# Moving the scaled and biased logits of a stick-breaking attention from ScalarE to VectorE

## The chip, the cores and the metric

The kernel runs on one core of one Trainium2 chip. The metric is the device time of one execution in microseconds (us), as the median of several executions. Engine names in the profile: PE is TensorE, DVE is VectorE, ACT is ScalarE, POOL is GpSimd, SP is SyncE.

## The reference

One inference step of a decoder with two layers, for 512 prompt tokens and 32 new tokens of 8 sequences, all in float32. Layer 0 is a recurrent block, layer 1 an attention block. The change touches only the attention over the prompt, which in the reference is:

```
z = einsum('bqkgd,bskd->bkgqs', qb, k) / sqrt(HEAD_DIM)      # HEAD_DIM = 128
z = z + bias[None, :, :, None, None]                          # one bias per head
mask = kpos[None, :] < qpos[:, None]                          # strictly causal
log_keep = where(mask, log_sigmoid(-z), 0.0)
suffix = cumsum(log_keep, axis=4, reverse=True) - log_keep
attn = where(mask, exp(log_sigmoid(z) + suffix), 0.0)
o = einsum('bkgqs,bskd->bqkgd', attn, v)
```

There are 16 heads in 4 groups (k = 0..3) of 4 heads (g = 0..3) that share one key and value head.

## The kernel before

**Tiling.** Every dense matrix product is done in three float32r passes (weights high x input high, high x low, low x high). The weights come in units of eight 128x128 tiles (512 KB). For each unit SP issues the DMA into `raw`, POOL multiplies it by the gain of a norm (`fold`, L633), ACT rounds it to a high part (`high`, L1197), DVE takes the rest as the low part (`low`, L1647), and PE multiplies the unit. `raw` and `WS` have two slots: SP may load a slot again when the `low` of that slot is done, so the time of a `low` sets the time of a later DMA and with it of a later `fold`. A unit takes PE about 6 us when nothing is put in between.

**The attention stage.** Loop `for n in range(D_UNITS)` runs over 64 weight units of the layer-1 projections. The 64 attention steps over the prompt are put in between by hand: a step is (k, g, s), where s = 0..3 picks one block of 128 keys, from the last to the first, and the queries from `FIRST_Q[s]` on: 256, 256, 384 and 512 of them. Sixteen steps of one k fall on 14 units from n = 7 + 14k on, most units with one step; the units n = 13 + 14k and n = 16 + 14k hold two, (s = 2, s = 3), and are called double units here. Inside a unit PE has a fixed place for each part of a step: the query-key product of the step after (`qk`) and the second part of the running sum (`rest`) in the first third, or after the first and the fifth tile in a double unit; the value product of the step before (`pv`, L912 to L914) and the running sum (`later`, L890 and L891) at the end, or in the middle and at the end of a double unit.

**One step** goes through the engines so:

- PE: `qk` writes the raw logits to `Z[:, 0, s % 2]` in PSUM.
- ACT, `exp_logits`: T1 = |scale z + bias| (L1377), T0 = scale z + bias (L1378), both read from PSUM; then T1 = exp(-T1) (L1380) and T1 = ln(1 + T1) (L1381).
- DVE, `softplus`: T3 = min(T0, 0) - T1 (L1934), T2 = max(T0, 0) + T1 (L1935), and a mask on T2 (L1937).
- ACT, `sp_split` (L1407), and DVE, `sp_rest` (L1942): high and low part of T2, which PE's `later` sums.
- DVE, `exponent` (L1948): T3 minus the sum in PSUM. ACT, `exp_arg` (L1389): exp of it. DVE, `mask_weights` (L1953). ACT, `at_split` (L1397), and DVE, `at_rest` (L1958): high and low part of the weights, which PE's `pv` takes.

**The order is written out by hand on each engine.** On ACT a step is `exp_arg` of the step before; for s = 0 `exp_logits` of this step; `at_split` of the step before; `sp_split`; and for s < 3 `exp_logits` of the next step. On DVE it is:

```
                if before:
                    exponent(*before)
                if next_unit is not None:
                    low(D0 + next_unit, next_unit % 2)
                if before:
                    mask_weights(*before)
                if s == 1 and (k or g):
                    head_out(*((k, g - 1) if g else (k - 1, GRP - 1)))
                softplus(k, g, s)
                if before:
                    at_rest(*before)
                sp_rest(k, g, s)
```

In an even unit DVE first takes the finished strip of the projection out of PSUM (`strip`, L1975 to L1978 or L1990); after the step come the low parts of a query or key strip (`q_rest`, L2010, `k_rest`, L2015), and in some odd units the gate product `silu` (L2001 to L2005). `gate_sigmoid` on ACT (L1443) loads another table set before and after its activation (the loads are at L1443 and L1445). It stands ahead of the step in n = 8 + 14k, and, for the gate strips behind the heads, in n = 58, 60 and 62. Behind the last step (n = 63) the paged decode attention begins, with its own logits (`logits`, L2079: scale and bias of a 128x512 PSUM tile on DVE).

Of the kernel before, what the change touches and what calls it, by code (L numbers as in the profile page):

```python
# [26 lines left out]
ALU = mybir.AluOpType  # L27
ACT = mybir.ActivationFunctionType
# [4 lines left out]
SEQ = 512  # L33
# [12 lines left out]
NH, NKV, GRP = 16, 4, 4  # L46
# [4 lines left out]
SCALE = DH ** -0.5  # L51
# [75 lines left out]
def build(nc, a, out):  # L127
    ctx = ExitStack()
    with ctx:
        def sem(name):  # L130
            return ctx.enter_context(nc.semaphore(name))
# [4 lines left out]
        def sb(name, shape, dt=F32, offset=None):  # L136
            size = 4
            for n in shape[1:]:
                size *= n
            if offset is None:  # L140
                offset = at[0]
                at[0] += (size + 31) // 32 * 32
            return nc.alloc_sbuf_tensor_at(name, list(shape), dt, offset=offset), offset
# [8 lines left out]
        T, T_AT = sb("T", [P, 12, 572])  # L152
# [10 lines left out]
        BIAS, _ = sb("BIAS", [P, NH])  # L163
# [34 lines left out]
        Z = ctx.enter_context(nc.psum_tensor("Z", [P, 2, 2, 512], F32))  # L198
# [6 lines left out]
        bias_in = sem("bias_in")  # L205
# [17 lines left out]
        sgb_ready = sem("sgb_ready")  # L223
        silu_done = sem("silu_done")
        qk_done = sem("qk_done")
        z_abs = sem("z_abs")
        z_out = sem("z_out")
        l_ready = sem("l_ready")
        sp_ready = sem("sp_ready")
# [164 lines left out]
        FIRST_Q = (2 * P, 2 * P, P, 0)  # L394
# [794 lines left out]
        def _(act):  # L1189
# [17 lines left out]
            steps = Steps(act, act_step)  # L1207
# [161 lines left out]
            def exp_logits(k, g, s):  # L1369

                n = k * 16 + 4 * g + s
                q = slice(FIRST_Q[s], SEQ)
                act.wait_ge(qk_done, n + 1)
                if n:
                    act.wait_ge(sp_ready, n)
                bias = BIAS[:, k * GRP + g:k * GRP + g + 1]
                nc.scalar.activation(T[:, 1, q], Z[:, 0, s % 2, q], ACT.Abs, scale=SCALE, bias=bias).then_inc(z_abs, 1)  # L1377
                nc.scalar.activation(T[:, 0, q], Z[:, 0, s % 2, q], ACT.Identity, scale=SCALE, bias=bias).then_inc(z_out, 1)  # L1378
                act.wait_ge(z_abs, n + 1)
                steps.done(nc.scalar.activation(T[:, 1, q], T[:, 1, q], ACT.Exp, scale=-1.0))  # L1380
                nc.scalar.activation(T[:, 1, q], T[:, 1, q], ACT.Ln, bias=1.0).then_inc(l_ready, 1)  # L1381

# [64 lines left out]
            def step(k, g, s):  # L1447
                before = (k, g, s - 1) if s else (k, g - 1, 3) if g else (k - 1, GRP - 1, 3) if k else None
                if before:
                    exp_arg(*before)  # L1450
                if s == 0:
                    exp_logits(k, g, 0)
                if before:
                    at_split(*before)
                sp_split(k, g, s)
                if s < 3:
                    exp_logits(k, g, s + 1)
# [45 lines left out]
                act.wait_ge(silu_done, GATES.index((o // GRP, o % GRP)) + 1)  # L1503
                nc.scalar.activation(U[:, o, 0:SEQ], Y[:, o, 0:SEQ], ACT.Copy).then_inc(y2_high, 1)

            act.wait_ge(bias_in, 16)
            for n in range(D_UNITS):
                j = n - PAGES_AT
                if 0 <= j < NHALF:
# [12 lines left out]
                kind, k, g = STRIPS[n // 2 - 1] if n >= 2 and n % 2 == 0 else (None, 0, 0)  # L1522
# [117 lines left out]
        def _(dve):  # L1640
            steps = Steps(dve, dve_step)
            V = nc.vector

            def low(m, slot, tiles=UT):

                dve.wait_ge(w_high, m + 1)
                V.tensor_tensor(WS[:, slot, 1, 0:tiles, :], raw[:, slot, 0:tiles, :],  # L1647
                                WS[:, slot, 0, 0:tiles, :].bitcast(F32), ALU.subtract).then_inc(w_low, 1)
# [271 lines left out]

            later_sum, o_sum = Z[:, 1, 0], Z[:, 1, 1]

            def masked_part(tile, s):

                q0 = FIRST_Q[s]
                return (tile[:, q0:q0 + 2 * P], MSK[:, :]) if s == 0 else (tile[:, q0:q0 + P], MSK[:, P:2 * P])

            def softplus(k, g, s):

                n = k * 16 + 4 * g + s  # L1930
                q = slice(FIRST_Q[s], SEQ)
                dve.wait_ge(l_ready, n + 1)
                dve.wait_ge(z_out, n + 1)
                V.scalar_tensor_tensor(T[:, 3, q], T[:, 0, q], 0.0, T[:, 1, q], ALU.min, ALU.subtract)  # L1934
                steps.done(V.scalar_tensor_tensor(T[:, 2, q], T[:, 0, q], 0.0, T[:, 1, q], ALU.max, ALU.add))  # L1935
                part, mask = masked_part(T[:, 2], s)
                V.tensor_tensor(part, part, mask, ALU.mult).then_inc(sp_ready, 1)  # L1937

            def sp_rest(k, g, s):
                q = slice(FIRST_Q[s], SEQ)  # L1940
                dve.wait_ge(sp_high, k * 16 + 4 * g + s + 1)
                V.tensor_tensor(U[:, 37, q], T[:, 2, q], U[:, 36, q].bitcast(F32), ALU.subtract).then_inc(sp_low, 1)  # L1942

            def exponent(k, g, s):

                q = slice(FIRST_Q[s], SEQ)
                dve.wait_ge(later_done, k * 16 + 4 * g + s + 1)
                V.tensor_tensor(T[:, 3, q], T[:, 3, q], later_sum[:, q], ALU.subtract).then_inc(arg_ready, 1)  # L1948

            def mask_weights(k, g, s):  # L1950
                dve.wait_ge(at_exp, k * 16 + 4 * g + s + 1)
                part, mask = masked_part(T[:, 4], s)
                V.tensor_tensor(part, part, mask, ALU.mult).then_inc(at_masked, 1)  # L1953

            def at_rest(k, g, s):
                q = slice(FIRST_Q[s], SEQ)
                dve.wait_ge(at_high, k * 16 + 4 * g + s + 1)
                V.tensor_tensor(U[:, 39, q], T[:, 4, q], U[:, 38, q].bitcast(F32), ALU.subtract).then_inc(at_low, 1)  # L1958

            def head_out(k, g):  # L1960

                dve.wait_ge(pv_done, k * 16 + 4 * g + 4)
                y = Y[:, k * GRP + g, 0:SEQ]
                if g:
                    V.tensor_copy(y, o_sum).then_inc(o_out, 1)
                else:
                    V.tensor_tensor(y, y, o_sum, ALU.mult).then_inc(o_out, 1)
# [53 lines left out]
            def step(k, g, s, next_unit):  # L2021
                before = (k, g, s - 1) if s else (k, g - 1, 3) if g else (k - 1, GRP - 1, 3) if k else None
                if before:
                    exponent(*before)
                if next_unit is not None:
                    low(D0 + next_unit, next_unit % 2)
                if before:
# [4 lines that stand above are left out]
                if before:  # L2032
                    at_rest(*before)
                sp_rest(k, g, s)
            def key_copy(c):
                dve.wait_ge(kp_t, c + 1)
                if c >= 4:
                    dve.wait_ge(kp_used, c - 3)
                V.tensor_copy(KPT[:, c % 4, :], KT).then_inc(kp_odd, 1)  # L2039
# [60 lines left out]
            for n in range(D_UNITS):  # L2100
# [3 lines left out]
                kind, k, g = STRIPS[n // 2 - 1] if n >= 2 and n % 2 == 0 else (None, 0, 0)  # L2104
# [3 lines left out]
                for t, step_ in enumerate(STEPS_AT.get(n, ())):  # L2108
                    step(*step_, next_unit if t == 0 else None)
# [16 lines left out]
                if 0 <= j < NHALF:  # L2126
                    key_copy(4 * j + 1)
# [14 lines left out]
                if 0 <= j < NHALF:  # L2142
                    key_copy(4 * j + 3)
                    logits(j)
# [115 lines left out]
```

## Time and profile before

| | |
|---|---|
| time, median of 3 executions | 1854.16 us (1853.96 to 1854.96) |
| time of the profiled execution | 1854.96 us |
| span of the profiled execution, first to last instruction | 1853.1 us |
| PE busy | 1741.2 us, 94% |
| DVE busy | 1095.8 us, 59% |
| ACT busy | 841.8 us, 45% |
| POOL busy | 250.4 us, 14% |
| attention steps over the prompt | 940 to 1418 us of the span |

The profile is of one execution. Busy time is a union of the instructions' times on an engine. A matmul is pipelined: one takes some 290 ns from start to end, and the next starts some 125 ns after it at full clock. The number in brackets behind a row of the timeline is how long the engine had been idle before the instruction, and whose end ended it.

### The profile page before, as it was taken

The page shows a single profiled execution, that of the slowest core. Times are in us where ns is not written, and L with a number is a line of the kernel's source. Part 1 is how long each engine was busy: PE and PEld are TensorE (multiplying, and loading weights), DVE is VectorE, ACT ScalarE, POOL GpSimd, SP SyncE. Part 2 cuts the span into 40 slices and gives each one's busy share as a digit, 9 for nine tenths or more (in the row PEclk, how much of TensorE's full clock was granted, in tenths as well). Part 3 has the DMA queues.
Part 4 walks back from the last instruction along what each step waited for, and adds up shares of the span by engine and source line. Part 5 has one row for each costly group of instructions (what it writes and reads, how often), then busy time and mean ns, then how long its engine had stood idle before and what let it go on. Part 6 is the DMA issues. An engine that isn't in the chain of part 4 may idle for free.

```text
span 1853.1 us, 35499 instructions
## 1 busy us (share of the span) xinstructions
PE 1741.2 (94%) x14003; PEld 1673.6 (90%) x14003; DVE 1095.8 (59%) x1853; ACT 841.8 (45%) x1310; POOL 250.4 (14%) x189
## 2 busy tenths in 40 slices
PE   6999999999999999994799999999988999999997
PEld 5999999999999999993698998998987888899995
DVE  4766555676557422229667677676676666642366
ACT  4434444334446222223256566665665555722343
POOL 2000000000000000013332232322311111001111
PEclk9999999999999999995699999999999999999997
DMA  8322332332332322334221222222223777622465
GB/s 243 109 86 75 90 91 81 88 102 70 89 91 57 91 85 85 90 115 144 88 82 59 57 83 58 80 69 58 81 57 100 213 225 222 200 76 84 135 185 181
DMA packets 293525, 197.97 MB, mean 107 GB/s; under 512 B 8379, under 2 KB 267579, under 8 KB 293307
## 3 DMA queue, kind: packets, MB, share of 16 engines
q1 hardware_dynamic: 290632, 187.36, 34.8%
q0 software_dynamic: 2720, 8.78, 1.3%
q8 instruction: 68, 1.11, 0.3%
q10 hardware_dynamic: 68, 0.41, 0.1%
q14 instruction: 37, 0.30, 0.1%
HBM read 180.55 MB, written 15.97 MB: 106 GB/s over the span
## 4 chain that ended last, share of the span: by engine, by line
PE 81%; DVE 9%; issue 4%; ACT 3%; DMA 1%; SPq 0%; POOL 0%; ACTq 0%; DVEq 0%
PE PS L722 23%; PE PS L724 23%; PE PS L723 23%; PE Z L972 2%; PE Z L722 2%; PE Z L724 1%; PE Z L723 1%; PE Z L982 1%; DMA xin<-in_x_prompt_dram 1%; DVE WS L1647 1%; PE Z L1006 1%; DVE T L1935 1%; DVE T L1934 1%; DVE Y L1903 1%; DVE U L1910 1%
## 5 line engine op out<-in xcount | busy, mean ns | idle before, releaser
L722 PE MATMUL PS<-U,WS 128*128 128x272 f32 x3680 | 1082.9, 294 | 48.2 <-DVE U L1910 34.1
L724 PE MATMUL PS<-U,WS 128*128 128x272 f32 x3680 | 1072.1, 291 | 0.0
L723 PE MATMUL PS<-U,WS 128*128 128x272 f32 x3680 | 1069.6, 291 | 0.0
L722 PEld LDWEIGHTS PS<-U,WS 128*128 128x128 f32 x3680 | 700.9, 190 | 61.1 <-issue 27.3
L723 PEld LDWEIGHTS PS<-U,WS 128*128 128x128 f32 x3680 | 701.6, 191 | 0.8
L724 PEld LDWEIGHTS PS<-U,WS 128*128 128x128 f32 x3680 | 700.8, 190 | 0.0
L1647 DVE TENSOR_TENSOR WS<-raw,WS 128x1024 fp32r<-128x1024 f32 (+1 forms) x223 | 272.3, 1221 | 381.4 <-ACT WS L1197 378.8
L1197 ACT ACTIVATE WS<-raw 128x1024 fp32r<-128x1024 f32 (+1 forms) x225 | 230.8, 1026 | 495.5 <-PE PS L724 492.0
L633 POOL TENSOR_TENSOR raw<-raw,GN 128x1024 f32<-128x1024 f32 x80 | 156.2, 1954 | 535.3 <-DMA raw<-in_b_w_in_dram 456.0
L645 POOL TENSOR_TENSOR T<-T 128x544 f32<-128x544 f32 x39 | 54.6, 1400 | 307.8 <-ACT T L1336 307.8
L642 POOL COPY T<-T 128x544 f32<-128x544 f32 x3 | 2.4, 791 | 623.2 <-ACT T L1336 573.8
L1407 ACT ACTIVATE U<-T 128x256 fp32r<-128x256 f32 (+1 forms) x64 | 32.0, 499 | 63.9 <-DVE T L1937 63.9
L1948 DVE TENSOR_TENSOR T<-T,Z 128x256 f32<-128x256 f32 (+1 forms) x64 | 33.2, 518 | 35.8 <-PE Z L891 35.1
L1397 ACT ACTIVATE U<-T 128x256 fp32r<-128x256 f32 (+1 forms) x64 | 31.7, 495 | 48.8 <-DVE T L1953 48.8
L1465 ACT ACTIVATE KPT<-Z 128x512 f32<-128x512 f32 x32 | 19.1, 598 | 74.7 <-PE Z L972 74.7
L2039 DVE COPY KPT<-Z 128x512 f32<-128x512 f32 x32 | 22.1, 691 | 50.4 <-PE Z L972 50.2
L1744 DVE SCALAR_TENSOR_TENSOR T<-T,CH 128x512 f32<-128x512 f32 x60 | 45.1, 752 | 7.7 <-DVE T L1742 2.6
L1336 ACT ACTIVATE T<-Y 128x544 f32<-128x544 f32 (+1 forms) x42 | 27.2, 647 | 48.7 <-DVE Y L1875 48.6
L724 PE MATMUL Z<-U,GWS 128*128 128x272 f32 x160 | 46.0, 288 | 0.0
L722 PE MATMUL Z<-U,GWS 128*128 128x272 f32 x160 | 45.9, 287 | 0.0
L723 PE MATMUL Z<-U,GWS 128*128 128x272 f32 x160 | 45.8, 286 | 0.0
L972 PE MATMUL Z<-IDN,KPG 128*128 128x128 f32 x256 | 41.9, 286 | 0.9 <-DMA KPG<-in_cache_k_dram 0.9
(284 smaller groups left out, 2062.2 us busy)
## 6 DMA issues: line engine op xcount, KB each, us to landing
raw<-in_a_w_in_dram SPq DMA_DIRECT2D x80, 512.0 KB, 3.8
raw<-in_b_w_in_dram SPq DMA_DIRECT2D x64, 512.0 KB, 4.1
raw<-in_a_w_out_dram SPq DMA_DIRECT2D x32, 512.0 KB, 3.8
KPG<-in_cache_k_dram SPq DMA_DIRECT2D x64, 256.0 KB, 3.1
raw<-in_b_w_out_dram SPq DMA_DIRECT2D x32, 512.0 KB, 3.9
VPG<-in_cache_v_dram SPq DMA_DIRECT2D x60, 256.0 KB, 3.0
RAW<-in_b_w_out_dram SPq DMA_DIRECT2D x12, 512.0 KB, 4.5
scratch_x<-T POOLq DMA_DIRECT2D x16, 272.0 KB, 3.5
```

Of the source, the lines that this page charges most:

```text
L633: pool.tensor_tensor(raw[:, slot], raw[:, slot], g, ALU.mult).then_inc(w_fold, 1)
L645: ins = pool.tensor_tensor(T[:, 6, 0:TOK], T[:, 6, 0:TOK], sq, ALU.add)
L722: pe.matmul(psum, w_hi, x_hi, start=first, stop=False)
L723: pe.matmul(psum, w_hi, x_lo, start=False, stop=False)
L724: return pe.matmul(psum, w_lo, x_hi, start=False, stop=last)
L972: ins = pe.transpose(KT[:, k * P:(k + 1) * P], KPG[j % 2][:, i, k * DH:(k + 1) * DH], IDN[:])
L1197: nc.scalar.activation(WS[:, slot, 0, 0:tiles, :], raw[:, slot, 0:tiles, :], ACT.Copy).then_inc(w_high, 1)
L1397: nc.scalar.activation(U[:, 38, q], T[:, 4, q], ACT.Copy).then_inc(at_high, 1)
L1407: nc.scalar.activation(U[:, 36, q], T[:, 2, q], ACT.Copy).then_inc(sp_high, 1)
L1647: V.tensor_tensor(WS[:, slot, 1, 0:tiles, :], raw[:, slot, 0:tiles, :], WS[:, slot, 0, 0:tiles, :].bitcast(F32), ALU.subtract).then_inc(w_ ...
L1744: V.scalar_tensor_tensor(xc[:, 0:SEQ], xp[:, k:k + SEQ], param(i, j, k), xc[:, 0:SEQ], ALU.mult, ALU.add)
L1948: V.tensor_tensor(T[:, 3, q], T[:, 3, q], later_sum[:, q], ALU.subtract).then_inc(arg_ready, 1)
```

## The change

T0 = scale z + bias is made by DVE as a `tensor_scalar` (a new function `scaled`), no longer by ACT as an Identity activation. ACT takes the absolute value of T0 in SBUF in place of its own pass over PSUM, and waits for `scaled` (semaphore `z_out`) where it waited for PE (`qk_done`); its exp now waits for its own absolute value just ahead of it. PE still waits for `z_out` before it writes a `Z` buffer again; the count is now raised by DVE. `scaled` for s = 0 stands on DVE behind `exponent` and ahead of `low`; for the other s it stands at the end of the step before, behind `sp_rest`. DVE waits in `scaled` for `qk_done` and for the ln of the step before. The semaphore `z_abs` goes, and so do DVE's wait for `z_out` in `softplus` and ACT's wait for the bias ahead of the loop (DVE has had one).

```diff
@@ scalar, exp_logits
-                act.wait_ge(qk_done, n + 1)
+                act.wait_ge(z_out, n + 1)
                 if n:
                     act.wait_ge(sp_ready, n)
-                bias = BIAS[:, k * GRP + g:k * GRP + g + 1]
-                nc.scalar.activation(T[:, 1, q], Z[:, 0, s % 2, q], ACT.Abs, scale=SCALE, bias=bias).then_inc(z_abs, 1)
-                nc.scalar.activation(T[:, 0, q], Z[:, 0, s % 2, q], ACT.Identity, scale=SCALE, bias=bias).then_inc(z_out, 1)
-                act.wait_ge(z_abs, n + 1)
+                steps.done(nc.scalar.activation(T[:, 1, q], T[:, 0, q], ACT.Abs))
                 steps.done(nc.scalar.activation(T[:, 1, q], T[:, 1, q], ACT.Exp, scale=-1.0))
                 nc.scalar.activation(T[:, 1, q], T[:, 1, q], ACT.Ln, bias=1.0).then_inc(l_ready, 1)
@@ scalar, ahead of the loop
-            act.wait_ge(bias_in, 16)
@@ vector
+            def scaled(k, g, s):
+                n = k * 16 + 4 * g + s
+                q = slice(FIRST_Q[s], SEQ)
+                dve.wait_ge(qk_done, n + 1)
+                if n:
+                    dve.wait_ge(l_ready, n)
+                V.tensor_scalar(T[:, 0, q], Z[:, 0, s % 2, q], SCALE, BIAS[:, k * GRP + g:k * GRP + g + 1],
+                                ALU.mult, ALU.add).then_inc(z_out, 1)
@@ vector, softplus
                 dve.wait_ge(l_ready, n + 1)
-                dve.wait_ge(z_out, n + 1)
@@ vector, step
                 if before:
                     exponent(*before)
+                if s == 0:
+                    scaled(k, g, 0)
                 if next_unit is not None:
                     low(D0 + next_unit, next_unit % 2)
@@ vector, end of step
                 sp_rest(k, g, s)
+                if s < 3:
+                    scaled(k, g, s + 1)
```

## Rows read from the trace of the kernel before

**Rows 1.** The page: span, and busy time of each engine.

```profile
span 1853.1 us, 35499 instructions
PE 1741.2 (94%) x14003; PEld 1673.6 (90%) x14003; DVE 1095.8 (59%) x1853; ACT 841.8 (45%) x1310; POOL 250.4 (14%) x189
```

**Rows 2.** Sums by window: stretch, length, busy PE PEld DVE ACT POOL, PE clock, DMA.

```profile
940.00:1418.00 478.00, 451.19 (x3357) 435.80 (x3360) 329.47 (x611) 301.31 (x557) 123.79 (x79) 0.99 0.25 71
```

**Rows 3.** Waits, 940 to 1418 us: who waited for whom, total us, times, longest.

```profile
PE Z L912 <- DVE U L1958: 14.6, 10, 2.2
...
PE Z L890 <- DVE U L1942: 4.7, 3, 2.8
```

**Rows 4.** One source line, the Identity activation: ns least/median/most.

```profile
L1378 ACT ACTIVATE T<-Z,BIAS x64: 462/518/684, 943.3 to 1404.5; 128x256 f32<-128x256 f32 x32, 128x384 f32<-128x384 f32 x16, 128x512 f32<-128x512 f32 x16
```

**Rows 5.** One source line, `logits` of the paged attention.

```profile
L2079 DVE TENSOR_SCALAR T<-Z,SM x16: 750/751/753, 1432.2 to 1608.5; 128x512 f32<-128x512 f32 x16
```

**Rows 6.** Timeline of the double unit n = 13: start us, length us, instruction.

```profile
995.53 0.56 DVE L1942 TENSOR_TENSOR U<-T,U 128x384 fp32r<-128x384 f32 x1 [0.26 <-ACT U L1407]
...
995.98 0.68 ACT L1378 ACTIVATE T<-Z,BIAS 128x512 f32<-128x512 f32 x1
...
996.54 0.63 ACT L1380 ACTIVATE T<-T 128x512 f32<-128x512 f32 x1
...
996.80 0.56 DVE L1948 TENSOR_TENSOR T<-T,Z 128x384 f32<-128x384 f32 x1 [0.71 <-PE Z L891]
...
997.20 0.63 ACT L1381 ACTIVATE T<-T 128x512 f32<-128x512 f32 x1
...
997.46 1.92 POOL L633 TENSOR_TENSOR raw<-raw,GN 128x1024 f32<-128x1024 f32 x1 [6.01 <-DMA raw<-in_w_v_dram]
...
997.74 0.51 ACT L1389 ACTIVATE T<-T 128x384 f32<-128x384 f32 x1
...
998.28 1.25 DVE L1953 TENSOR_TENSOR T<-T,MSK 128x128 f32<-128x128 f32 x1 [0.93 <-ACT T L1389]
...
1001.58 0.44 PE L912 MATMUL Z<-U,KVP 128*128 128x384 f32 x1 [1.30 <-DVE U L1958]
```

**Rows 7.** Timeline of the double unit n = 41.

```profile
1229.29 0.56 DVE L1942 TENSOR_TENSOR U<-T,U 128x384 fp32r<-128x384 f32 x1 [0.25 <-ACT U L1407]
...
1231.01 1.92 POOL L633 TENSOR_TENSOR raw<-raw,GN 128x1024 f32<-128x1024 f32 x1 [5.79 <-DMA raw<-in_w_v_dram]
```

**Rows 8.** Timeline of the double unit n = 58.

```profile
1375.29 1.94 DVE L1942 TENSOR_TENSOR U<-T,U 128x384 fp32r<-128x384 f32 x1 [0.25 <-ACT U L1407]
...
1378.54 0.52 ACT L1389 ACTIVATE T<-T 128x384 f32<-128x384 f32 x1 [0.95 <-DVE T L1948]
...
1381.62 0.69 DVE L1942 TENSOR_TENSOR U<-T,U 128x512 fp32r<-128x512 f32 x1 [0.23 <-ACT U L1407]
...
1383.16 0.40 PE L890 MATMUL Z<-U,TRI 128*128 128x512 f32 x1
```

**Rows 9.** Timeline, end of unit n = 61 and start of n = 62.

```profile
1405.34 0.69 DVE L2003 TENSOR_TENSOR Y<-Y,T 128x512 f32<-128x512 f32 x1
...
1405.95 1.92 POOL L633 TENSOR_TENSOR raw<-raw,GN 128x1024 f32<-128x1024 f32 x1 [6.79 <-DMA raw<-in_b_w_in_dram]
...
1407.37 0.72 DVE L1990 TENSOR_TENSOR T<-PS,RS 128x544 f32<-128x544 f32 x1 [1.35 <-PE PS L724]
```

**Rows 10.** Timeline, unit n = 12: the fold and the low part after it.

```profile
982.48 1.92 POOL L633 TENSOR_TENSOR raw<-raw,GN 128x1024 f32<-128x1024 f32 x1 [6.73 <-DMA raw<-in_w_k_dram]
...
983.23 2.25 DVE L1647 TENSOR_TENSOR WS<-raw,WS 128x1024 fp32r<-128x1024 f32 x1
```

**Rows 11.** Timeline, end of the first step's unit, n = 7.

```profile
950.04 0.38 PE L890 MATMUL Z<-U,TRI 128*128 128x256 f32 x1 [2.79 <-DVE U L1942]
...
950.91 1.04 ACT L1197 ACTIVATE WS<-raw 128x1024 fp32r<-128x1024 f32 x1
```

**Rows 12.** Sums by window behind that unit, columns as in rows 2.

```profile
951.00:954.00 3.00, 3.00 (x15) 3.00 (x14) 1.22 (x1) 2.95 (x5) 0.35 (x1) 0.52 0.35 98
```

More of the change, by code:

```diff
@@ L225, in build @@
         qk_done = sem("qk_done")
-        z_abs = sem("z_abs")
         z_out = sem("z_out")
```

## Prediction

> **What bounds the kernel now.** The page comes first: PE is busy for 94% of the span, DVE for 59%, ACT for 45% [rows 1], so a change on DVE and ACT can only move the time where PE waits for them. The windows narrow that to the stage that the change touches: in the 478 us of the attention steps PE is busy for 451.2, so 26.8 us are idle, while DVE is busy for 329.5 and ACT for 301.3 [rows 2]. Neither is full; what counts is the order of single instructions. The waits say which: PE idles before `pv` for DVE's `at_rest` ten times, 14.6 us, and before `later` for DVE's `sp_rest` three times, 4.7 us [rows 3]. Then the timeline around these places, above all in the double units, where two steps share one unit; seven of the eight look like n = 13 [rows 6].
>
> There the order is to be read. After `sp_rest` of s = 2 (995.53) DVE idles 0.71 us until `exponent` (996.80), which waits for PE. ACT meanwhile makes Identity, exp and ln of s = 3 and gets to `exp_arg` at 997.74, whose end (998.25) lets DVE's mask L1953 start at 998.28. That mask of 128 columns takes 1.25 us. The reason is POOL: its fold runs from 997.46 to 999.38, and the mask ends 0.15 us behind it, at 999.53 [rows 6]. So a DVE instruction with two SBUF inputs that starts under a fold waits for the fold's end. A `low` in n = 12 shows the same: it starts at 983.23 under the fold of 982.48, and ends at 985.48, 1.08 us behind the fold's end [rows 10]. In the double units, therefore, the end of the chain (mask, `softplus`, `at_rest`, and then PE, idle for 1.30 us) is set by the fold, not by ACT. The Trainium skill (SBUF — State Buffer, "Who interferes with whom") says that a DVE instruction with two SBUF inputs contends with a GpSimd instruction that reads SBUF, and that the later one fully blocks; the trace agrees.
>
> **The change part by part.** *ACT loses 64 Identities*: 64 x 0.518 = 33 us of busy time [rows 4]. *DVE gains 64 `tensor_scalar`*. The same operation on a 512-column PSUM tile takes 0.751 us [rows 5]; for 384 and 256 columns I take 0.62 and 0.48, by the step of 0.13 per 128 columns between 512 (0.69) and 384 columns (0.56) of DVE's own instructions [rows 6, 8]. 16 x 0.75 + 16 x 0.62 + 32 x 0.48 = 37 us. DVE's busy time in the stage goes to about 366 of 478 us, ACT's to 268. Neither sum is in the time by itself. *The waits removed* (bias, `z_out` in `softplus`) end long before their place, and cost nothing either way.
>
> *Seven double units.* `sp_rest` starts at 995.53 and is 0.56 long; instructions without a wait overlap by some 0.09 (ln at 997.20, 0.63 long, `exp_arg` at 997.74), so `scaled` of s = 3 runs from 996.01 to 996.76. That fits into DVE's idle 0.71 us with 0.04 to spare, and `exponent` stays at 996.80 [rows 6]. ACT can only start its absolute value at 996.79. An activation that waits for the one ahead starts 0.66 later (996.54 to 997.20), one that doesn't 0.54 later: exp 997.45, ln 998.11, `exp_arg` 998.65, end 999.16, mask 999.19. ACT's chain gets later by 0.91 us, though it has an instruction less, since it starts after DVE's `sp_rest` and `scaled`. But the fold lasts until 999.38, 3.85 us behind the start of `sp_rest`, and the chain now needs 3.66: the mask still ends at 999.53. Price 0. The shortest such distance of the seven is in n = 41: 1229.29 to 1232.93, 3.64 us [rows 7]; there the mask starts 0.02 late and runs its own 0.3 instead of 0.15 behind the fold: +0.2. Sum +0.2. From below: 0, since the fold stands where it is (its DMA hangs on a `low` ahead of all this). From above: a chain 0.3 us longer than worked out passes the folds by some 0.15 to 0.3 in each, +2.0. If the cover were gone on both sides, each would cost 0.91.
>
> For the absolute value I take exp's 0.63, SBUF to SBUF; read from PSUM an activation of that size takes 0.68 [rows 6]. The Trainium skill (VectorE: DVE Perf Modes, the section on the TRN2 errata) has it the other way round, ACT with a fixed cost of 224 cycles from SBUF and 172 from PSUM. By that the absolute value would take 0.68 + 0.04 and each chain be 0.09 longer, which the fold still covers in six of the seven.
>
> *n = 58*, the eighth double unit, has no such cover: its `sp_rest` is itself held by a fold, until 1377.23. `scaled` then ends at 1377.90, and `exp_arg` starts at 1377.93 + 0.66 + 0.66 + 0.54 = 1379.79 instead of 1378.54, 1.25 later. `sp_rest` of s = 3 moves by as much, from 1381.62 to 1382.87, and ends at 1383.56; PE wanted to start `later` at 1383.16 [rows 8]. +0.4 (0 to 1.2).
>
> *End of n = 61.* `scaled` of s = 3 (0.75 long, 0.67 for what follows) stands ahead of `silu`. Its last product starts at 1405.34, 0.6 ahead of the fold (1405.95); 0.67 later it comes behind it and is held until 1407.87 + 0.53 = 1408.40 [rows 9]. `strip`, due at 1407.37, moves by nearly 1 us, and with it the gate's sigmoid and the step behind it, part of which another hold takes up. +0.5 (0 to 1.0).
>
> *`low` for s = 0* starts 0.4 later, behind `scaled`. Softplus of that step comes a little earlier in exchange (ACT is one instruction shorter where it doesn't wait for DVE). Where nothing else holds that `low`, its DMA and the next unit's fold come 0.4 later. The fold of 982.48 already holds a `low` [rows 10]; it would hold it 0.4 longer, and with it the double unit behind. I count two of the four k (in the others a fold holds the late `low` anyway): +0.8 (0 to 1.6).
>
> *n = 7.* ACT is an instruction shorter there, `softplus` 0.3 earlier, so PE's idle 2.79 us shrink by 0.2 to 0.6. But ACT's next `high`, at 950.91 [rows 11], now stands behind a chain that waits for DVE's `sp_rest` and `scaled`, some 0.2 later, and sets the next fold. +0.2, at most +0.5. From below −0.6, and the clock: behind this idle time it is 0.52 for 3 us [rows 12], the lower of its levels of 1.2 and 2.4 GHz. If it stayed up, some 1.5 us more would come back: −2.1.
>
> Sum: 0.2 + 0.4 + 0.5 + 0.8 + 0.2 = +2.1 us. On the profiled execution, 1854.96, that is 1857.1; that execution lies 0.8 above the median, so I forecast 1854.16 + 2.1 = 1856.3.
>
> **The rivals.** *Late `low`, slower.* DVE's `low` is late by 0.4 in each s = 0 unit but the first of a k, where DVE waits for `high` anyway: twelve. If every such delay passes through DMA and fold to PE, it costs 12 x 0.4 = 4.8 instead of 0.8, so +6.1: 1860.3. For it: the chain from `low` through DMA to fold is fixed, and folds hold DVE [rows 6, 10]. Against: most units have idle time on all three engines, PE waits in few of them [rows 3]. It decides where the fold of the next unit starts ahead of the `low` that it holds. A rule stands behind this side too: the Trainium skill (Perfetto Trace Analysis, "Optimizing Scalar/DVE Operations") moves work off DVE if DVE is saturated, and this change moves it onto the busier engine.
>
> *ACT's relief reaches PE, faster.* If PE's waits in the eight double units hung on ACT's chain, and `scaled` were done as soon as ACT comes free, each would lose one Identity, 0.56 us (995.98 to 996.54): −4.5, 1849.7. Against: DVE is in `sp_rest` at that moment, and the mask ends with the fold [rows 6].
>
> *The first stall gives way, no change.* The lower bound of n = 7 comes true, the clock stays up, the rest as summed: 2.1 − 2.3 = −0.2: 1854.0.
>
> **How the numbers follow.** Chances: forecast 0.56, late `low` 0.26, faster by ACT 0.08, first stall 0.10. 0.2%, about what a measurement of this kernel tells from no change, is 3.7 us: 1850.5 to 1857.9. The forecast's own bounds are 1852.0 (n = 7 at −2.1, all others at 0) and 1860.5 (+2.0, 1.2, 1.0, 1.6, 0.5), most of it below 1857.9; of its 0.56 I give 0.07 to slower, as several terms would have to be at their upper ends. Faster 0.09 (with 0.01 of the first stall), same 0.58 (0.49 + 0.09), slower 0.33. Range 1851.0 to 1860.8, which leaves out the rival of ACT and the far end of the late `low`; the likeliest case's own range is 1852 to 1860.5.
>
> **What would show it.** ACT's busy time down by some 33 us, DVE's up by some 37. `scaled` of 512 columns 0.75 long. In n = 13 `exponent` less than 0.1 behind the end of `scaled`; `exp_arg` 3.1 us behind the start of `sp_rest` instead of 2.2; the mask still ending 0.15 behind the fold, and PE's idle time before L912 still 1.3. In n = 58 a new short wait before L890. At the end of n = 61 L2003 held by a fold. Wrong it would be if `scaled` were itself held by folds, if the folds moved away from the masks, or if PE's waits before L912 changed by more than 0.3 in each double unit.

## The result and the profile after

The changed kernel took 1867.66 us (median of 5 executions, 1865.51 to 1870.97) against 1854.96 us before (5 executions, 1853.96 to 1862.42): 1.0059 times as long, 95% interval 1.0036 to 1.0084. It is slower, by 7 to 16 us (the ratio is not that of the two medians, 1.0068); forecast were 1856.3 us, with a range up to 1860.8. The profiled execution took 1867.35 us.

The page of the kernel after, to be held against [rows 1]:

```profile
span 1865.6 us, 35498 instructions
...
PE 1744.6 (94%) x14003; PEld 1675.2 (90%) x14003; DVE 1119.7 (60%) x1917; ACT 820.3 (44%) x1246; POOL 251.6 (13%) x189
```

The span is 12.5 us longer. DVE has 24 us more and ACT 21.5 us less, and both still idle 40% and more of the time. Forecast were 37 more and 33 less. The 64 new instructions do take 37.0 us; but other instructions of DVE were held less than before (the mask on the weights by 6.1 us in all, `q_rest` by 5.5), and those of ACT overlap less. One line of the source, the new operation; its three sizes take 0.48, 0.61 and 0.745 us (forecast 0.48, 0.62 and 0.75):

```profile
L1924 DVE TENSOR_SCALAR T<-Z,BIAS x64: 470/544/747, 941.1 to 1414.2; 128x256 f32<-128x256 f32 x32, 128x384 f32<-128x384 f32 x16, 128x512 f32<-128x512 f32 x16
```

Sums by window from the first `later` of the attention to that of its last step, (3,3,3); first the kernel before, then after (columns as in [rows 2]):

```profile
950.04:1416.96 466.92, 442.90 (x3267) 428.11 (x3268) 322.84 (x605) 296.47 (x549) 118.29 (x76) 0.99 0.24 70
```
```profile
949.52:1426.91 477.39, 447.67 (x3268) 430.06 (x3268) 346.19 (x668) 275.45 (x487) 119.91 (x77) 0.99 0.24 68
```

The stage is 10.5 us longer: PE idles 29.7 us in it instead of 24.0, and is busy for 4.8 us more with the same matmuls. The start of the stage is 0.5 us earlier, and what lies behind it takes 2.5 us more. So the loss is in and just behind the steps. The waits of 940 to 1418 us (who waited for whom, total us, times, longest), after, with [rows 3] as the other side:

```profile
PE Z L911 <- DVE U L1961: 13.0, 9, 2.6
...
ACT WS L1196 <- PE PS L723: 8.3, 8, 4.5
PE Z L889 <- DVE U L1945: 6.2, 4, 2.0
...
PE Z L897 <- DVE T L1951: 5.5, 8, 1.5
```

Two rows of before in the same view:

```profile
ACT WS L1197 <- PE PS L724: 29.3, 36, 4.5
...
PE Z L898 <- DVE T L1948: 3.5, 7, 1.4
```

PE's wait before `pv` (L911; L912 before), around which the prediction was built, has not grown. The row that moved most is one of ACT: `high` used to be in place early 36 times and wait for PE's release; now it does so 8 times. In the other cases ACT itself comes late. And PE waits longer at `rest` (L897, for `exponent`), a place that the prediction never priced.

**Inside a double unit the forecast holds.** Timeline of n = 13 after, beside [rows 6]:

```profile
995.26 0.56 DVE L1945 TENSOR_TENSOR U<-T,U 128x384 fp32r<-128x384 f32 x1 [0.26 <-ACT U L1403]
995.74 0.74 DVE L1924 TENSOR_SCALAR T<-Z,BIAS 128x512 f32<-128x512 f32 x1
996.51 0.63 ACT L1375 ACTIVATE T<-T 128x512 f32<-128x512 f32 x1 [1.29 <-DVE T L1924]
996.53 0.55 DVE L1951 TENSOR_TENSOR T<-T,Z 128x384 f32<-128x384 f32 x1
996.84 1.92 POOL L632 TENSOR_TENSOR raw<-raw,GN 128x1024 f32<-128x1024 f32 x1 [5.89 <-DMA raw<-in_w_v_dram]
...
998.38 0.51 ACT L1385 ACTIVATE T<-T 128x384 f32<-128x384 f32 x1
998.92 0.29 DVE L1956 TENSOR_TENSOR T<-T,MSK 128x128 f32<-128x128 f32 x1 [1.83 <-ACT T L1385]
```

`exponent` follows the end of `scaled` by 0.05, `exp_arg` stands 3.12 behind the start of `sp_rest` (forecast 3.1), and the mask starts 3.66 behind it (forecast 3.66). The fold comes 0.35 earlier than in [rows 6] and no longer holds the mask, which now takes 0.29, so that it ends 3.95 behind `sp_rest` instead of 4.00. In the seven double units the mask took 1.0 to 1.45 us before and takes 0.3 to 0.7 now: the later chain has used up nearly all the cover of the folds, as forecast.

**What stands behind the chain on ACT.** Timeline from n = 54 into the double unit n = 55, after:

```profile
1345.08 0.43 DVE L1945 TENSOR_TENSOR U<-T,U 128x256 fp32r<-128x256 f32 x1
1345.42 0.61 DVE L1924 TENSOR_SCALAR T<-Z,BIAS 128x384 f32<-128x384 f32 x1
1346.07 0.53 ACT L1375 ACTIVATE T<-T 128x384 f32<-128x384 f32 x1 [1.02 <-DVE T L1924]
...
1347.62 0.61 ACT L1431 ACTIVATE U<-T 128x512 fp32r<-128x512 f32 x1
...
1348.26 0.69 DVE L2013 TENSOR_TENSOR U<-T,U 128x512 fp32r<-128x512 f32 x1 [2.23 <-ACT U L1431]
1348.87 0.41 DVE L1951 TENSOR_TENSOR T<-T,Z 128x256 f32<-128x256 f32 x1
...
1349.34 0.38 PE L897 MATMUL Z<-U,TRI 128*128 128x256 f32 x1 [1.49 <-DVE T L1951]
```

The same place before:

```profile
1340.42 0.62 ACT L1435 ACTIVATE U<-T 128x512 fp32r<-128x512 f32 x1
1341.07 1.51 DVE L2010 TENSOR_TENSOR U<-T,U 128x512 fp32r<-128x512 f32 x1 [2.00 <-ACT U L1435]
...
1342.50 0.41 DVE L1948 TENSOR_TENSOR T<-T,Z 128x256 f32<-128x256 f32 x1
...
1342.96 0.39 PE L898 MATMUL Z<-U,TRI 128*128 128x256 f32 x1 [0.36 <-DVE T L1948]
```

After, ACT's absolute value waits for `scaled`, which waits behind `sp_rest`. `q_split` (L1431) stands behind exp and ln of that chain, DVE's `q_rest` (L2013) waits 2.23 us for it (2.00 before), `exponent` stands behind `q_rest`, and PE waits 1.49 us for `exponent` (0.36 before). But e_early, an experiment below in which ACT's chain is not late, has an even longer wait at this place:

```profile
1342.47 0.38 PE L897 MATMUL Z<-U,TRI 128*128 128x256 f32 x1 [1.79 <-DVE T L1951]
```

e_s0, level with before as well, has 1.84 there. So the order on ACT does make `rest` wait, but this place does not show that the change lengthened the wait.

**The distances.** From each step's `later` to the next one's, in us, added up by place from the start times in the traces. The first two columns are the kernels before and after; the others are experiments, below.

```
place (distances)                     before  after   e_s0  e_s123 e_wait h_split e_early h_before h_early2
step of n = 8 (1)                       9.55  10.24   7.51  10.24  10.24  10.29    7.51    7.51    7.50
s = 3 after g = 0, s = 0 of g = 1 (8)  60.79  62.08  60.79  62.11  61.42  62.05   60.78   60.80   60.77
first step of a double unit (7)        37.75  39.09  39.42  39.39  41.67  36.63   40.89   34.53   37.82
second step of a double unit (7)       44.76  44.97  44.68  45.35  43.35  45.20   43.19   44.62   42.58
next step after it (7)                 56.11  59.10  56.13  57.62  56.13  57.67   56.14   57.63   56.12
double unit n = 58 (2)                 14.66  15.49  15.46  15.61  15.29  15.69   15.30   15.66   15.37
last four steps (4)                    33.80  36.40  33.81  35.12  36.91  35.76   34.11   33.81   33.79
others (27)                           209.50 210.02 209.81 209.82 209.78 209.44  210.32  209.33  210.18
sum                                   466.92 477.39 467.61 475.26 474.79 472.73  468.24  463.89  464.13
```

The +10.5 of after are 3.0 behind the double units, 2.6 in the last four steps, 1.3 at the start of double units, 1.3 in the units where a `high` is late (two distances of every k, +0.23 and +0.10, the same in all four k), 0.8 in n = 58, 0.7 in n = 8, and 0.7 elsewhere.

One profile does not carry all of these. h_early and h_early2 are one kernel, profiled twice: h_early has 36.68 for the first steps of the double units, 14.54 for n = 58 and 35.86 for the last four steps, where h_early2 has 37.82, 15.37 and 33.79. Differences of 1 to 2 us in these rows can be scatter. Three places are beyond it. The seven profiles in which the chains of s > 0 start late have 10.23 to 10.36 in n = 8, and the seven others besides that of before have 7.50 to 7.51. The last distance alone, from (3,3,2) to (3,3,3), is 11.41 to 13.36 in the six profiles in which the chain started in n = 60 is late, and 9.43 to 9.76 in the nine others. The second row is 62.0 to 62.1 in five of the seven late ones (61.4 and 62.7 in the other two), and 60.8 in all the rest.

The 3.0 behind the double units are two distances, 9.54 and 9.46 us where before has 8.01 and 8.02. There the granted clock is lower. One stretch at one of them, after, and the same stretch before:

```profile
1030.00:1032.00 2.00, 2.00 (x10) 1.90 (x9) 1.52 (x3) 0.80 (x2) 0.00 (x0) 0.50 0.00 0
```
```profile
1030.00:1032.00 2.00, 2.00 (x17) 1.96 (x16) 1.79 (x3) 0.90 (x3) 0.00 (x0) 1.00 0.00 0
```

The clock is at the lower level of 1.2 GHz, and 10 matmuls start instead of 17. The kernel before had such a stretch in n = 8 [rows 12], of which after is free.

### The profile page after: what moved, and what is told of

Read it like the earlier page. It is cut to its first block, busy times and chain, and to the rows that moved or that the text cites. A ratio compares the mean times of both kernels' runs of the same rounds, so it can differ in the third digit from the quotient of the medians.

```text
span 1865.6 us, 35498 instructions
## 1 busy us (share of the span) xinstructions
PE 1744.6 (94%) x14003; PEld 1675.2 (90%) x14003; DVE 1119.7 (60%) x1917; ACT 820.3 (44%) x1246; POOL 251.6 (13%) x189
## 4 chain that ended last, share of the span: by engine, by line
PE 80%; DVE 10%; ACT 4%; issue 4%; DMA 1%; SPq 0%; POOL 0%; ACTq 0%; DVEq 0%
PE PS L721 23%; PE PS L723 22%; PE PS L722 22%; PE Z L971 2%; PE Z L721 1%; PE Z L723 1%; PE Z L722 1%; DVE WS L1642 1%; PE Z L981 1%; DMA xin<-in_x_prompt_dram 1%; PE Z L1005 1%; ACT U L1403 1%; DVE T L1938 1%; DVE T L1937 1%; DVE Y L1898 1%
## 5 line engine op out<-in xcount | busy, mean ns | idle before, releaser
L1642 DVE TENSOR_TENSOR WS<-raw,WS 128x1024 fp32r<-128x1024 f32 (+1 forms) x223 | 277.0, 1243 | 385.3 <-ACT WS L1196 382.9
L1375 ACT ACTIVATE T<-T 128x256 f32<-128x256 f32 (+1 forms) x64 | 31.7, 495 | 57.1 <-DVE T L1924 57.1
```

## The experiments

Thirteen runs of twelve kernels, each against the kernel before on the same chip. Ratios are of times, with the 95% interval. The theories: **A**, ACT's chain of s > 0 starts too late, behind DVE's `sp_rest` and `scaled`; **B**, the late `low` of s = 0; **C**, DVE's 37 us of new instructions as such; **D**, half-clock stretches that follow PE's idle times; **E** and **F**, what of A hits which instruction behind the chain.

**Which half of the steps (e_s0, e_s123).** The same code, with `scaled` on DVE only where the condition holds, and the old form elsewhere. As both engines now raise `z_out`, each also waits for the count of the step before. Against the kernel before, with parts left out (`...`):

```diff
+                if s == 0:          # e_s123: if s > 0
+                    act.wait_ge(z_out, n + 1)
...
+                    steps.done(nc.scalar.activation(T[:, 1, q], T[:, 0, q], ACT.Abs))
+                else:
+                    act.wait_ge(qk_done, n + 1)
...
+                    nc.scalar.activation(T[:, 1, q], Z[:, 0, s % 2, q], ACT.Abs, scale=SCALE, bias=bias).then_inc(z_abs, 1)
+                    nc.scalar.activation(T[:, 0, q], Z[:, 0, s % 2, q], ACT.Identity, scale=SCALE, bias=bias).then_inc(z_out, 1)
```

> The scaled logits are made by VectorE for s = 0 only; s = 1 to 3 stay as before. Theory A (the loss comes from the s > 0 steps, whose absolute value on ScalarE now starts behind VectorE's sp_rest and scaled): within 2 us of the kernel before. Theory B (the loss comes from the late low behind scaled of s = 0, as in the rival of the prediction): 5 us or more above the kernel before.

> The scaled logits are made by VectorE for s = 1 to 3 only; s = 0 stays as before. Theory A: 8 to 13 us above the kernel before, nearly all of the loss. Theory B: less than 5 us above it.

e_s0 took 1856.37 us against 1855.6, ratio 1.000 (0.999 to 1.001); e_s123 1866.18 us, ratio 1.0059 (1.0038 to 1.008). Within these intervals the whole loss belongs to s > 0. B, the prediction's slower rival, is out.

**The wait alone (e_wait).** The kernel before with one wait, so that DVE and ACT do the old work in the new order.

```diff
                 if n:
                     act.wait_ge(sp_ready, n)
+                if s:
+                    act.wait_ge(sp_low, n)
```

> The kernel before, with one wait more: for s > 0 ScalarE's exp_logits starts only when VectorE's sp_rest of the step before is done; no work is moved. Theory A (the later start of ScalarE's chain alone costs): 4 to 12 us above the kernel before. Rival C (what costs is the 37 us of instructions added to VectorE): within 2 us of it.

1864.1 us, ratio 1.0044 (1.0029 to 1.006). One wait, with nothing moved to DVE, costs some three quarters of the loss; the intervals do not tell the two losses apart. In the table its n = 8 is that of after (10.24), and its last four steps have 0.5 us more. The rest is not a copy of after: ACT still has its Identity here, the first steps of the double units have 3.9 us more than before (after 1.3), the second ones 1.4 less.

**ACT's relief alone (e_relief).** The Identity is left out, and nothing takes its place, so this kernel does not compute the attention over the prompt.

```diff
-                nc.scalar.activation(T[:, 1, q], Z[:, 0, s % 2, q], ACT.Abs, scale=SCALE, bias=bias).then_inc(z_abs, 1)
-                nc.scalar.activation(T[:, 0, q], Z[:, 0, s % 2, q], ACT.Identity, scale=SCALE, bias=bias).then_inc(z_out, 1)
-                act.wait_ge(z_abs, n + 1)
+                nc.scalar.activation(T[:, 1, q], Z[:, 0, s % 2, q], ACT.Abs, scale=SCALE, bias=bias).then_inc(z_out, 1)
+                act.wait_ge(z_out, n + 1)
```

> The kernel before without the Identity on ScalarE: the biased logits are not written, and softplus takes what lies in the tile, so the attention over the prompt is not computed; the waits stay. It shows what 33 us less on ScalarE are worth with nothing given to VectorE. Theory A and the prediction: 0 to 2 us below the kernel before, since the folds and PE's own order hold the chain. The rival of the prediction (ScalarE's relief reaches PE): 4 us or more below it.

1854.39 us, ratio 0.9999 (0.9985 to 1.0013). 33 us off ACT, with nothing given to DVE, bring less than the interval of some 2.5 us shows; the rival's 4.5 us are out.

**The same work, placed early (e_early).** After, with `scaled` of the next step ahead of `sp_rest`.

```diff
                 if before:
                     at_rest(*before)
+                if s < 3:
+                    scaled(k, g, s + 1)
                 sp_rest(k, g, s)
-                if s < 3:
-                    scaled(k, g, s + 1)
```

> The changed kernel with scaled of s + 1 ahead of sp_rest instead of behind it, so that ScalarE's absolute value can start some 0.6 us earlier; sp_rest starts up to 0.5 us later. Theory A (ScalarE's late chain holds q_split, high and exp_arg): at least 4 us below the changed kernel, 1855 to 1863. Rival: sp_rest, which PE's later waits for, costs what the chain gains: within 3 us of the changed kernel.

1857.72 us against 1856.97, ratio 1.0002 (0.9988 to 1.0016). All 64 new instructions are on DVE, and the loss is gone: A holds and C is out. This pair is the proof, since the two kernels differ in the order of two instructions alone. Where the time comes back is seen in n = 7 and 8. Timeline after:

```profile
947.83 1.65 DVE L1945 TENSOR_TENSOR U<-T,U 128x256 fp32r<-128x256 f32 x1 [0.48 <-ACT U L1403]
...
949.39 0.47 DVE L1924 TENSOR_SCALAR T<-Z,BIAS 128x256 f32<-128x256 f32 x1
...
951.12 1.04 ACT L1196 ACTIVATE WS<-raw 128x1024 fp32r<-128x1024 f32 x1
...
955.44 0.42 ACT L1385 ACTIVATE T<-T 128x256 f32<-128x256 f32 x1
...
957.43 2.00 POOL L632 TENSOR_TENSOR raw<-raw,GN 128x1024 f32<-128x1024 f32 x1 [5.68 <-DMA raw<-in_b_w_in_dram]
...
957.71 0.39 PE L911 MATMUL Z<-U,KVP 128*128 128x256 f32 x1 [0.87 <-DVE U L1961]
957.80 1.91 DVE L1945 TENSOR_TENSOR U<-T,U 128x256 fp32r<-128x256 f32 x1
...
959.76 0.39 PE L889 MATMUL Z<-U,TRI 128*128 128x256 f32 x1 [1.43 <-DVE U L1945]
```

The same in e_early:

```profile
946.99 2.08 POOL L632 TENSOR_TENSOR raw<-raw,GN 128x1024 f32<-128x1024 f32 x1 [0.76 <-DMA raw<-in_b_w_in_dram]
947.23 0.48 DVE L1924 TENSOR_SCALAR T<-Z,BIAS 128x256 f32<-128x256 f32 x1
...
947.79 1.57 DVE L1945 TENSOR_TENSOR U<-T,U 128x256 fp32r<-128x256 f32 x1
...
948.96 1.04 ACT L1196 ACTIVATE WS<-raw 128x1024 fp32r<-128x1024 f32 x1
...
953.28 0.42 ACT L1385 ACTIVATE T<-T 128x256 f32<-128x256 f32 x1
```

In after, a fold (947.28 to 949.19) holds `sp_rest` (1.65 us instead of 0.43), `scaled` and ACT's chain wait with it, and `high` and everything behind it on ACT come 2.16 us later than in e_early: `exp_arg` at 955.44 instead of 953.28. The next `sp_rest` then meets the next fold too, and PE waits 0.87 and 1.43 us. In e_early `scaled`, ahead of the same `sp_rest`, takes 0.48 under the fold.

**Filled idle times (f_after, f_before).** Matmuls without use ahead of `pv` in the double units and two (f_after) or three (f_before) other units, with the numbers of them per unit given below.

```diff
+            FILL = {13: 9, 16: 9, 27: 9, ..., 7: 14, 62: 20}     # f_before: 7: 20, 60: 8, 62: 14
+            def filler(n):
+                for _ in range(FILL.get(n, 0)):
+                    pe.matmul(PS[:, (n // 2 + 1) % 2, 0, HALF:HALF + 2 * P - 16], TRI[:, 0, :], ...)
```

> The changed kernel with matmuls of no use (240 columns, into unused PSUM columns) ahead of pv at the end of the eight double units (9 each), of n = 7 (14) and n = 62 (20), where PE idles for VectorE. Theory D (some 5 us of the loss are stretches at half clock behind PE's idle times: four more of some 1.7 us each, in 1029, 1149, 1426 and 1436 us, and one less): with the idle times filled these stretches go, 4 to 8 us below the changed kernel. Against D: no gain, or a loss of up to 3 us by the added matmuls.

> The kernel before with the same fillers (9 in each double unit, 20 in n = 7, 8 in n = 60, 14 in n = 62). Theory D: its two stretches at half clock in the attention stage (951 and 1378 us) go, 1 to 4 us below the kernel before. Against D: no gain, or a loss of up to 3 us.

f_after 1868.47 us, ratio 1.0062 (1.0044 to 1.008); f_before 1857.11 us, ratio 1.0005 (0.9994 to 1.0016), both against 1856.97. Filling moved neither, so D was not borne out. It is not excluded either. In f_after's trace the distances behind the double units are back at 56.1 us and the last four steps at 34.3, but the first steps of the double units have 44.3 instead of 39.1, with PE idle at `rest`, which was left unfilled, for 2.5 us in n = 27 and 2.7 in n = 55. What came back in one place was lost in another, and why was not settled.

**The end of n = 61 (g_silu).** After, with `scaled` behind `silu` in the two odd units of the last head, as the prediction's step on n = 61 would have it.

```diff
-                if s < 3:
+                if s < 3 and (k, g, s) not in ((3, 3, 0), (3, 3, 2)):
                     scaled(k, g, s + 1)
...
                     silu(*STRIPS[n // 2 - 1][1:])
+                if STEPS_AT.get(n, ())[-1:] in ([(3, 3, 0)], [(3, 3, 2)]):
+                    scaled(3, 3, STEPS_AT[n][-1][2] + 1)
```

> The changed kernel with scaled behind silu instead of ahead of it in n = 59 and n = 61. The prediction put 0.5 us on silu being pushed under a fold there; the trace of the changed kernel shows no hold at L2006, and the last step's value product still 2 us later. If silu is the cause: those 2 us go, and step (3,3,3) lies as far behind step (3,3,2) as before (9.44 us between their later products). Theory E (the cause is ScalarE's chain of n = 60, late behind a sp_rest held by a fold, and high and low behind it): nothing moves by more than 0.5 us there. Total within 3 us of the changed kernel either way.

1870.51 us against 1856.55, ratio 1.0075 (1.0048 to 1.0102). The last distance grew from 11.93 to 13.36 us instead of falling to the 9.44 of before. `silu` is not what the loss there hangs on; the trace of after also shows its L2006, the former L2003, at its own 0.69 us, not held. That the distance grew by 1.4 us was not expected by E either, which had put at most 0.5: here `scaled` itself starts behind `silu`, at 1417.35 us, and PE waits 4.54 us for the `pv` ahead of the last `later`.

**One step early (l_331).** After, with `scaled` ahead of `sp_rest` only in step (3,3,1), n = 60.

```diff
+                if (k, g, s) == (3, 3, 1):
+                    scaled(k, g, s + 1)
                 sp_rest(k, g, s)
-                if s < 3:
+                if s < 3 and (k, g, s) != (3, 3, 1):
                     scaled(k, g, s + 1)
```

> The changed kernel with scaled ahead of sp_rest in one step alone, (3,3,1) in n = 60. Theory E: high of n = 61 no longer waits for that chain, and the 2 us at the end of the attention stage go: the later products of (3,3,2) and (3,3,3) lie some 9.5 us apart, as before and as in the version with all scaled ahead of sp_rest. Otherwise: some 11.9 us apart, as in the changed kernel. Total 1863 to 1867.

The last distance is 9.44 us, that of before, though `scaled` still stands ahead of `silu` in n = 61. The total, 1867.66 us, ratio 1.005 (1.0028 to 1.0071), lies above the expected 1863 to 1867 and cannot show 2.5 us. E holds for the distance. The timeline of after, n = 60 to 63, says how:

```profile
1404.81 2.16 POOL L632 TENSOR_TENSOR raw<-raw,GN 128x1024 f32<-128x1024 f32 x1 [5.14 <-DMA raw<-in_b_w_in_dram]
...
1405.35 1.90 DVE L1945 TENSOR_TENSOR U<-T,U 128x256 fp32r<-128x256 f32 x1
1407.17 0.60 DVE L1924 TENSOR_SCALAR T<-Z,BIAS 128x384 f32<-128x384 f32 x1
...
1407.81 0.53 ACT L1375 ACTIVATE T<-T 128x384 f32<-128x384 f32 x1 [2.50 <-DVE T L1924]
...
1409.36 1.04 ACT L1196 ACTIVATE WS<-raw 128x1024 fp32r<-128x1024 f32 x1
...
1410.43 1.23 DVE L1642 TENSOR_TENSOR WS<-raw,WS 128x1024 fp32r<-128x1024 f32 x1 [2.16 <-ACT WS L1196]
...
1425.78 0.69 PE L911 MATMUL Z<-U,KVP 128*128 128x384 f32 x1 [2.87 <-DVE U L1961]
```

The fold holds `sp_rest`, it holds `scaled`, ACT idles 2.50 us, `high` follows the chain, and `low` waits 2.16 us for `high`. Two units later PE idles 2.87 us (1.90 before).

**`q_split` ahead of the chain (h_split, h_early).** ACT's `q_split` stands ahead of `exp_logits` of the next step, once in after (h_split) and once in e_early (h_early).

```diff
                 sp_split(k, g, s)
+                if ahead:
+                    ahead()            # q_split of this unit
                 if s < 3:
                     exp_logits(k, g, s + 1)
```

> The changed kernel with ScalarE's q_split ahead of exp_logits of the next step instead of behind it. Theory F (in n = 12 + 14k q_split, q_rest and with them exponent and PE's rest of the double unit are late behind ScalarE's chain): PE's idle times before rest at the start of n = 27, 41 and 55 (0.66, 0.27 and 1.49 us) fall below 0.3 each; total 1 to 3 us below the changed kernel. Against F: they stay.

> scaled ahead of sp_rest and q_split ahead of exp_logits, together. The first alone took back all of the loss; if q_split still costs there (PE's idle times before rest in n = 27, 41 and 55 grew by 0.2 to 1.7 us in it), 1 to 3 us below the kernel before: 1852 to 1855. Otherwise: as the kernel before.

h_split 1860.88 us, ratio 1.0027 (1.0013 to 1.0041); h_early 1853.55 us, ratio 0.9983 (0.9971 to 0.9994), against 1856.55. The first steps of the double units go from 39.09 to 36.63 us, `high`'s eight distances stay at 62.05, and PE's waits at `rest` in n = 27, 41 and 55 are gone: the order of `q_split` costs time there, and the late `high` is a loss of its own. Whether the change brought the first of these costs is for the next pair to say.

**The order alone (h_before, h_early2).** The same edit in the kernel before, beside h_early once more.

> The kernel before with one edit alone: ACT's q_split stands ahead of exp_logits of the next step, as in h_split. Theory F (q_split and with it DVE's q_rest come late in the units that a double unit follows, and PE's rest behind them) also speaks of the kernel before: PE's idle time ahead of rest at the start of n = 13 + 14k, 1.38, 0.23, 0.38 and 0.36 us there, goes to about 0, and the time falls by 2 to 3 us, to a ratio of 0.9985 or so; then what h_early gained is the order of q_split and not the scaled logits on DVE. Rival: the kernel before gains nothing from it (ratio 0.9995 to 1.0005), since ACT's exp_logits then starts behind q_split; then h_early's gain comes from the scaled logits on DVE.

> The version of h_early once more, on the same chip as h_before. If the order of q_split is all, its ratio lies within 0.001 of that of h_before. If the scaled logits on DVE bring something of their own where they stand early, it lies more than 0.001 below it. Also a second reading of 0.9983.

h_before 1852.05 us against 1855.03, ratio 0.998 (0.9968 to 0.9992); h_early2 1853.42 us, ratio 0.9991 (0.9977 to 1.0004). The waits of 940 to 1418 us in h_before, to be held against `rest`'s 3.5 us above:

```profile
PE Z L898 <- DVE T L1951: 0.3, 2, 0.2
```

The order of `q_split` beats the kernel before by itself. With the scaled logits on DVE on top the ratio is no lower (0.0011 higher, a little more than the 0.001 that was expected at most, with intervals that overlap), so h_early's gain is that of the order. The best version found is h_before, without the change.

h_before and h_split also are a pair: both have the new order of `q_split`, and only the second has the change. Between them lie 0.0047, against 0.0059 between before and after. In the table it is 8.8 us: 2.8 in n = 8, 2.1 and 0.6 in the first and second steps of the double units, 2.0 in the last four steps, 1.3 where a `high` is late, and nothing behind the double units. So most of the loss is there whichever way `q_split` stands, and F is a weakness that the kernel before already had.

## Why the prediction was wrong

**What held.** The durations and ACT's chain: 0.74 us for 512 columns, 3.12 and 3.66 us behind `sp_rest`. The double units from `sp_rest` to `pv`: +0.2 forecast, and the second steps of the seven have +0.21 (44.97 against 44.76). ACT's relief brings nothing measurable, as its rival was judged (e_relief).

**What came out by luck.** n = 58: +0.4 forecast, +0.83 found, inside its bounds; but the new short wait of PE before the second `later`, which was to make it, is not in the trace (1390.51 us, no idle time), and h_before, without the change, has 15.66 in that row, more than after. n = 7 and 8: +0.2 forecast, −0.52 + 0.69 = +0.17 found, by a balance that was not foreseen. The first idle time shrank to 2.02 us, and the clock stayed up (a window like that of [rows 12] has 1.00). Against that stands the chain: every version with it behind `sp_rest` has 10.24 us or more in n = 8, every one in the table without it has 7.5, except the profiled execution of before, 9.55 with the clock at 0.52 for a while. So the rival of the first stall had its condition come true and not its gain. The prediction saw that ACT's `high` would stand behind the chain there, but took the chain to be 0.2 us late; with `sp_rest` held by a fold `high` is 2.16 us later than in e_early, and the term is +2.7 us where no stretch at half clock is in the way.

**The step that failed** is the stop behind "Price 0". The price itself fits the seven double units: there the folds covered the chain. But the prediction found that ACT's chain of s > 0 gets 0.91 us later, followed it to `exp_arg` in the eight double units, saw it covered there, and stopped. What else is queued behind `exp_logits` on ACT it asked in n = 7 alone (`high`, priced at +0.2), and it put the other 39 of the 48 chains of s > 0 at nothing without a reason. What the runs showed in its place is the late `high`, which makes `low` and all that stands behind it on DVE late: +2.7 in n = 8, +2.0 to +2.5 in the last distance, and +1.3 in the same two distances of each k, each back to 0.3 or less in e_early. That is 6.0 to 6.5 us of some 11 to 13. That it is `high` among the instructions behind the chain is read from the timelines; no run moved `high` alone. `q_split` is queued there too and makes `q_rest`, `exponent` and PE's `rest` late. Moving it took 0.0032 off the changed kernel, but 0.0020 off the kernel before as well, so only the smaller part of that can be the change's, and +1.3 in the first steps of the double units is hardly beyond the scatter.

**The terms that were mis-sized** are n = 7 (above) and the end of n = 61, +0.5 against +2.5 in the last distance. The mechanism of the second was wrong: not `silu` behind a fold (g_silu made it worse) but `sp_rest` of n = 60 held by a fold, and `scaled`, the chain, `high` and `low` behind it (l_331). The prediction knew that a fold holds `sp_rest`; it used this for n = 58 alone.

**`low` for s = 0**, +0.8, and the rival built on it, +6.1: e_s0 is level within 0.1% either way, 1.9 us, so +0.8 is neither shown nor excluded, and +4.8 is out. In its trace the first steps of the double units have +1.7, n = 58 +0.8, and n = 8 −2.0; which of these is `low`'s was not separated.

**DVE's load.** The Trainium skill (Perfetto Trace Analysis, "Optimizing Scalar/DVE Operations") moves work off DVE where DVE is saturated. It is not here (60% busy), and the runs agree that load was not the matter: 64 more instructions on DVE gave 1.0002, one wait without them 1.0044.

**What stays open.** Of the profiled +12.5 us some 5 lie at half clock: 3.0 in the two distances behind double units, and 2 behind the stage, where 1426.91 to 1452 us has a granted clock of 0.82. Such stretches change place from one profile to the next: e_s123 has one behind a double unit, but at another (n = 56), e_wait has none there, and h_before and e_relief, which are not slower than before, have one each. Yet their total goes with the late chain: from 930 to 1700 us the granted clock is at its lower level for 20.5 to 27.3 us in the six profiles with it and without fillers, and for 10.2 to 17.1 us in the seven without both. f_after has 13.7 us, and its time did not fall. Whether this is a part of the loss or goes along with it was not settled. Without these 5 us, 7.5 us are left, or 9.5 if n = 8 of before is taken at the 7.5 us of the other kernels; both lie inside the 7 to 16 us of the timing.

## What to carry to other kernels

An instruction moved to another engine takes its place in that engine's queue, and the first engine now waits for everything ahead of that place; write down all that is queued behind the waiting instruction, in every unit of the loop, not only where PE waits now. If the new producer must stand behind something, put it ahead of whatever another engine can hold. Before moving work, run the wait alone: it costs one line, and here it showed some three quarters of the loss, if partly at other places. And compare an experiment with the same edit in the kernel before: without h_before, h_early would have passed for a gain of the change.

## What the runs showed that was not expected

`scaled`, a DVE instruction that reads its tile from PSUM, was not held by POOL's fold: for 256 columns it took 0.48 us at 947.23 in e_early, wholly under the fold from 946.99 to 949.07, while the two-input `sp_rest` at 947.79 took 1.57 and ended behind it. None of the six that started under a fold in e_early took longer than the others of its size. So `scaled` stood safely ahead of `sp_rest`, and was at its mercy behind it. An absolute value from SBUF took 0.63 us for 512 columns, where the Identity from PSUM had taken 0.68 [rows 6], in the order that the prediction had assumed. Stretches at half clock were in every kernel; between 930 and 1700 us they were 3.4 to 13.7 us long.
